# Turning the probabilities of two attentions with operands in the rounded format, in a three-layer float32 kernel

## The chip, the cores and the metric

The kernel runs on one core of a Trainium2 chip. The metric is the device time of one execution in microseconds (us); lower is better. The core's engines run side by side and order their work by semaphores: TensorE (PE, with its weight loads PEld), VectorE (DVE), ScalarE (ACT), GpSimd (POOL) and SyncE (SP, which issues most transfers).

## What is computed

All in float32, for one sequence of 1024 tokens with 1024 channels. First two layers that add an attention branch and a Fourier branch:

```python
for l in range(2):
    h = rms_norm(x, norm_g[l])
    c_q, c_kv, k_pe, z_a, u_f, z_f, g_a, g_f = split(h @ w_in[l])
    q, k, v = heads(c_q, c_kv, k_pe)            # 8 heads, 96 for q and k, 64 for v, norms and rotation
    p = softmax(q @ k.T * 96 ** -0.5)           # no mask, 1024 x 1024 for each head
    y_a = ((p @ v) * silu(z_a)) @ w_attn_proj[l]
    y_f = (real(fft2(u_f)) * silu(z_f)) @ w_fourier_proj[l]
    x = x + (sigmoid(g_a) * y_a + sigmoid(g_f) * y_f) @ w_out[l]
```

Then one hybrid layer. An indexer scores the visible keys of each query, the best 256 are kept, and 8 heads attend to their shared latents (128 wide, causal); beside it runs a state-space branch. The two are joined, projected with `w_out`, added to the scaled input and layer-normed:

```python
s = where(kept, q_lat @ c.T, -big)
out = (softmax(s) @ c) @ w_uv
y = concat([out * silu(gate_a), ssm * silu(gate_s)]) @ w_out
return layer_norm(2 ** 0.25 * x + y, ln_g, ln_b)
```

## The kernel before

Every engine has its own instruction stream, written out by hand in order; semaphores tie the streams together, and the eight PSUM banks (`PS[:, b, :]`, 128 x 512) pass between PE and its readers by a pair of semaphores each (`full`, `free`). SBUF regions are reused from stage to stage under new names. A helper, `sb2`, lays out one region under two names: a plain float32 view (`R2b`) and a view in the rounded format, float32r (`R2bR`). Products that are wide enough are split: an operand is rounded (the high part), the rest is a second operand, and three matmuls in the rounded format take the place of one in plain float32. The trace prints both formats as f32 for PE; the names with R, Hi or Lo are the rounded ones.

The first attention takes 64 units a layer (8 heads of 8 blocks of 128 queries). For unit u PE runs, in this order: `scores(u + 1)` (L597, six matmuls of 128 x 512 into two banks), every second time `pv_pair` (L621, the products with v of two units, 32 matmuls), at four steps a head a `qk_turn` (L579, four turns of the next head's q and k), and `p_turn(u)` (L607, eight turns of 128 x 128 into banks 4 and 5). DVE takes the maximum of the scores (L1813), ACT the exponential into `Pb[u % 2]` (L1375), and DVE and ACT copy the turned blocks to SBUF (L1821, L1822, L1826, L1368). During the last head ACT and DVE also round and split h for the products that follow (L1349, L1353, L1801).

The second attention goes block by block of queries (t from 0 to 7), eight heads each. `scores2` (L990) and `p_turn2` (L1002) treat only the t + 1 visible key blocks, so it has 288 turns; `latent_out` (L1012), `att_out` (L1022), `att_turn` (L1030) and `out_half` (L1043, the output projection of the block before) stand between them. At the end DVE adds the residual, subtracts the mean (L2206, L2208), ACT takes square and root (L1600, L1601), and `layer_norm` (L2216 and the two steps behind it, L1972 and L2218) finishes block 7, which SP writes out.

A turn is `pe.transpose(out, in, ident)`: a load of a stationary operand of 128 columns and a matmul that moves 128 columns, of the block and the identity. All turns of the kernel use one tile, `ident`, in plain float32.

At the start SP loads four constants (`ident`, `dft_d`, `cosT`, `sinT`, L1075 to L1078), each adding 16 to `s_const`; PE, DVE and POOL wait for 64. ACT issues the loads of x and begins with `x_std` (L1256, L1257): squares and root for each block of x; DVE normalises (L1673), PE turns (L478), DVE copies into `hT` (L1693), and PE projects (L488).

Of the kernel before, what the change touches and what calls it, by code (L numbers as in the profile page):

```python
# [7 lines left out]
ALU = mybir.AluOpType  # L8
ACT = mybir.ActivationFunctionType
AX = mybir.AxisListType  # L10
F32 = mybir.dt.float32

F32R = mybir.dt.float32r

P = 128
S = 1024
D = 1024
NT = S // P
# [122 lines left out]
def build(nc, a, out):  # L142

    with ExitStack() as ctx:
        def sb(name, shape, dt=F32):
            return ctx.enter_context(nc.sbuf_tensor(name, shape, dt))

        def sb2(name, rounded, shape):

            with nc.sbuf_tensor(name, shape, F32) as plain:  # L150
                pass
            return plain, sb(rounded, shape, F32R)
# [11 lines left out]
        R2b, R2bR = sb2("R2b", "R2bR", [P, 4, 1024])  # L164
        R3a, R3aR = sb2("R3a", "R3aR", [P, 4, 1024])
        R3b, R3bR = sb2("R3b", "R3bR", [P, 4, 1024])
        W, WR = sb2("W", "WR", [P, W_SLOTS, KD * C_COLS])
        ident = sb("ident", [P, P])
        dft_d = sb("dft_d", [P, 2 * P])
        u_mid = sb("u_mid", [P, FG, P])  # L170
        cosT = sb("cosT", [P, NT, HR])
# [8 lines left out]
        ssc = sb("ssc", [P, 2 * NT])  # L180
# [30 lines left out]
        v_tok = r1[:, 4096:8192].rearrange("p (t h c) -> p t h c", t=NT, h=H)  # L211
        r2a = R2a[:, :, :].rearrange("p a b -> p (a b)")
        Pb = [R2b[:, 0, :], R2b[:, 1, :]]
        PT = [R2b[:, 2, :], R2b[:, 3, :]]

        qkT = [[R3aR[:, i, :], R3aR[:, 2 + i, :]] for i in range(2)]
# [23 lines left out]
        def flat(t):  # L240
            return t[:, :, :].rearrange("p a b -> p (a b)")
# [64 lines left out]
        wukT = CT.rearrange("p i q c -> p (i q c)").rearrange("p (m c) -> p m c", m=4)  # L306
        wuv = Bb.rearrange("p i q c -> p (i q c)").rearrange("p (h d) -> p h d", h=H)
        qlT = R0
        Pb2 = [r3b[:, 0:1024], r3b[:, 1024:2048]]
        xt = [r3b[:, 2048:3072], r3b[:, 3072:4096]]  # L310
        lng, lnb = r3a[:, 0:1024], r3a[:, 1024:2048]
# [2 lines left out]
        PT2 = [hTf[:, i * 4096:(i + 1) * 4096].rearrange("p (k c) -> p k c", k=NT) for i in range(2)]  # L314
# [7 lines left out]
        full = [sem(f"bank_full{b}") for b in range(8)]  # L322
# [3 lines left out]
        s_const = sem("constants_loaded")  # L326
# [118 lines left out]
        @block.tensor  # L445
        def _(pe):
            bk = Banks(full, free)
            pe.wait_ge(s_const, 64)
            pe.wait_ge(s_init, 3)

            def begin(b):
# [12 lines left out]
            for l in range(L):  # L464
# [5 lines left out]
                for i, (what, t) in enumerate(START):  # L470
                    b = start_banks(i)
                    if what == "x":
                        pe.wait_ge(s_xn, l * NT + t + 1)
                        for j in range(2):
                            o = begin(b[j])
                            for k in range(4):
                                f = 4 * j + k
                                mm = pe.transpose(o[:, k * P:(k + 1) * P], xn[t][:, f * P:(f + 1) * P], ident[:, :])  # L478
# [6 lines left out]
                    for j, (lo, hi) in enumerate(((0, QL + ROPE), (QL + ROPE, C_COLS))):  # L485
                        o = begin(b[j])
# [5 lines left out]
                for m in range(4):  # L492
                    pe.wait_ge(s_uwlo, l * 4 + m + 1)
                    for n in range(2):
                        b = 2 * m + n
                        o = begin(b)
# [13 lines left out]
                for t in range(NT):  # L510
                    pe.wait_ge(s_cn, l * NT + t + 1)
                    o = begin(t % 8)
# [88 lines left out]
                def p_turn(u):  # L601
                    pe.wait_ge(free[2 * (u % 2)], bk.count(2 * (u % 2)))
                    for j in range(2):
                        o = begin(4 + j)
                        for k in range(4):
                            c = 4 * j + k
                            mm = pe.transpose(o[:, k * P:(k + 1) * P], Pb[u % 2][:, c * P:(c + 1) * P], ident[:, :])  # L607
                        mm.then_inc(full[4 + j], 1)
                    pt_count.append((bk.count(4), bk.count(5)))

# [383 lines left out]
            def p_turn2(u):  # L994
                t = u // H
                pe.wait_ge(free[2 * (u % 2)], bk.count(2 * (u % 2)))
                for j in range(2):
                    if 4 * j > t:
                        continue
                    o = begin(4 + j)  # L1000
                    for c in range(4 * j, min(4 * j + 4, t + 1)):
                        mm = pe.transpose(o[:, (c % 4) * P:(c % 4 + 1) * P], Pb2[u % 2][:, c * P:(c + 1) * P], ident[:, :])  # L1002
                    mm.then_inc(full[4 + j], 1)
                pt2[u] = (bk.count(4), bk.count(5))

# [28 lines left out]
            def out_half(t, n, half):  # L1034

                if (n, half) == (1, 0):
                    pe.wait_ge(free[6], turn_free[0])
                    if t == 0:
                        pe.wait_ge(s2_glu, 8)
                wo = k_of(weights2(6 + n)) if t == half == 0 else k_of(W[:, n, :])  # L1040
                o = begin(6 + n) if half == 0 else PS[:, 6 + n, :]
                for k in range(4 * half, 4 * half + 4):
                    mm = pe.matmul(o, mix[:, k, t * P:(t + 1) * P], wo[:, k, :], start=(k == 0), stop=(k == 7))  # L1043
                if half == 1:
                    mm.then_inc(full[6 + n], 1)
# [22 lines left out]
            att_turn(NT - 1)  # L1068
            for i in range(4):
                out_half(NT - 1, 1 - i // 2, i % 2)  # L1070

        @block.sync
        def _(sp):
            sp.dma_start(ident[:, :], a["c_ident"]).then_inc(s_const, 16)  # L1075
            sp.dma_start(dft_d[:, :], a["c_dft_d"]).then_inc(s_const, 16)
            sp.dma_start(cosT[:, :, :], a["c_cos"].rearrange("(t p) c -> p t c", p=P)).then_inc(s_const, 16)
            sp.dma_start(sinT[:, :, :], a["c_sin"].rearrange("(t p) c -> p t c", p=P)).then_inc(s_const, 16)  # L1078
# [161 lines left out]
        def _(act):  # L1240
            bk = Banks(full, free)
            st = Steps(act, s_act)
            for t in range(NT):
                act.dma_start(x1[:, t, :], a["x"][0, t * P:(t + 1) * P, :]).then_inc(s_xin[t], 16)
            act.wait_ge(s_init, 3)

            def arrive(b):
                act.wait_ge(full[b], bk.take(b) + 1)
# [396 lines left out]
        def _(dve):  # L1645
# [6 lines left out]
            dve.memset(rows[:, :], 0.0).then_inc(s_init, 1)  # L1652
            dve.memset(u_mid[:, :, :], 0.0).then_inc(s_init, 1)
            dve.wait_ge(s_init, 3)
            dve.wait_ge(s_const, 64)

            def arrive(b):
                dve.wait_ge(full[b], bk.take(b) + 1)
# [312 lines left out]
            def stt(out_, in0, c, in1, op0, op1):  # L1971
                st.link(dve.scalar_tensor_tensor(out=out_, in0=in0, scalar=c, in1=in1, op0=op0, op1=op1))  # L1972
# [219 lines left out]
            def residual(t, n):  # L2192

                x = xt[t % 2]
                if n == 1:
                    dve.wait_ge(s2_xt[t % 2], 16 * (t // 2 + 1))
                o = arrive(6 + n)
                xx = x[:, n * 512:(n + 1) * 512]
                dve.scalar_tensor_tensor(out=xx, in0=xx, scalar=ALPHA, in1=o, op0=ALU.mult, op1=ALU.add
                                         ).then_inc(free[6 + n], 1)  # L2200
                if n == 1:
                    half_free[t] = bk.count(7)
                    return
                dve.wait_ge(free[7], half_free[t])
                dve.wait_ge(free[6], bk.count(6))
                st.link(dve.tensor_reduce(ssc[:, NT + t:NT + t + 1], x, AX.X, ALU.add))  # L2206
                ts(ssc[:, NT + t:NT + t + 1], ssc[:, NT + t:NT + t + 1], -1.0 / D, None, ALU.mult)
                dve.tensor_scalar(x, x, ssc[:, NT + t:NT + t + 1], None, ALU.add).then_inc(s2_r, 1)  # L2208
# [3 lines left out]
            def layer_norm(t):  # L2212
                x = xt[t % 2]
                dve.wait_ge(s2_ln, 32)
                dve.wait_ge(s2_sq, t + 1)
                st.link(dve.reciprocal(rsx[:, t:t + 1], rsx[:, t:t + 1]))  # L2216
                stt(x, x, rsx[:, t:t + 1], lng, ALU.mult, ALU.mult)
                dve.tensor_tensor(x, x, lnb, ALU.add).then_inc(s2_o, 1)  # L2218

            def turned(u):  # L2220
# [53 lines left out]
            layer_norm(NT - 2)  # L2274
            residual(NT - 1, 1)
            residual(NT - 1, 0)
            layer_norm(NT - 1)

        @block.gpsimd  # L2280
        def _(pool):
            bk = Banks(full, free)
            st = Steps(pool, s_pool)
            q3 = q_tok.rearrange("p t (h c) -> p t h c", h=H)
            pool.wait_ge(s_const, 64)
            for l in range(L):
                for n in ROUND[:7]:
                    bk.skip(n)
# [275 lines left out]
```

## Time and profile before

| | us |
|---|---|
| median of 3 runs (2581.4 to 2584.61) | 2583.34 |
| the profiled execution's own time | 2583.04 |
| its span in the trace | 2581.2 |
| PE busy, share of the span | 2463.0, 95% |
| DVE busy | 1420.3, 55% |
| ACT busy | 837.0, 32% |
| POOL busy | 389.9, 15% |

The span runs from the first to the last instruction of the profiled execution; what the own time has beyond it lies around the program. Busy times of PE are those of pipelined matmuls whose ends are modelled, so the start of one matmul to the start of the next says more than the length of one; a run of matmuls in the chain of waits gives it, as the length of the run over their count. PEld rows are the loads of the stationary operand, which overlap PE. The chain of waits is the chain of work that ended last, followed back from the end.

### The profile page before, as it was taken

The numbers are of one execution on the slowest core, as the hardware profiler recorded it, in microseconds if no ns is written. First come the engines' busy times: TensorE is split into PE (matmuls) and PEld (weight loads), VectorE is DVE, ScalarE is ACT, GpSimd is POOL, SyncE is SP. The second block draws the span as 40 slices with busy tenths as digits, with TensorE's granted clock in tenths as the row PEclk, the third lists the DMA queues.
The fourth block names the chain that finished last, engine by engine and source line by source line (L and its number), as shares of the span: only waits on it lengthen the run. The fifth ranks groups of instructions, "written<-read, shape, count | busy, mean of one in ns | idle before, by whom it ended". The sixth has DMA issues, their size and how long they took to land.

```text
span 2581.2 us, 30768 instructions
## 1 busy us (share of the span) xinstructions
PE 2463.0 (95%) x12425; PEld 1802.1 (70%) x12425; DVE 1420.3 (55%) x2274; ACT 837.0 (32%) x1478; POOL 389.9 (15%) x491
## 2 busy tenths in 40 slices
PE   6999998999999999999989999999999999989997
PEld 5867887788777787688868887776557455644553
DVE  2365777342223243477762322243689999977762
ACT  3344455231113142345451311131351113423341
POOL 0015230100000001233110000000233962300000
PEclk9999999999999999999999999999999999999999
DMA  5010000311113121000012111123011011200000
GB/s 205 29 50 1 2 1 1 92 36 46 42 49 131 49 84 46 33 1 2 1 35 56 49 49 50 57 98 101 39 40 35 1 43 41 98 17 33 17 25 25
DMA packets 106381, 116.82 MB, mean 45 GB/s; under 512 B 20704, under 2 KB 78784, under 8 KB 106240
## 3 DMA queue, kind: packets, MB, share of 16 engines
q1 hardware_dynamic: 105088, 110.66, 13.8%
q10 hardware_dynamic: 1152, 4.19, 0.4%
q8 instruction: 99, 1.62, 0.2%
q14 instruction: 42, 0.34, 0.0%
HBM read 96.82 MB, written 16.84 MB: 44 GB/s over the span
## 4 chain that ended last, share of the span: by engine, by line
PE 77%; DVE 18%; ACT 3%; issue 1%; SPq 1%; POOL 1%; DMA 0%; DVEq 0%; ACTq 0%
PE PS L656 7%; PE PS L659 7%; PE PS L662 7%; PE PS L597 6%; DVE R2a L2143 6%; DVE ssc L2142 5%; PE PS L488 5%; PE PS L621 4%; PE PS L607 4%; PE PS L1043 4%; PE PS L709 2%; PE PS L725 2%; PE PS L533 2%; PE PS L728 2%; PE PS L722 2%; PE PS L1012 2%
## 5 line engine op out<-in xcount | busy, mean ns | idle before, releaser
L656 PE MATMUL PS<-hHi,R2bR 128*128 128x512 f32 x768 | 301.7, 393 | 7.3 <-POOL hHi L2337 7.3
L659 PE MATMUL PS<-hLo,R2bR 128*128 128x512 f32 x768 | 300.7, 392 | 0.0
L662 PE MATMUL PS<-hHi,R2bR 128*128 128x512 f32 x768 | 300.5, 391 | 0.0
L1834 DVE TENSOR_TENSOR R2bR<-W,R2bR 128x1024 fp32r<-128x1024 f32 x48 | 61.9, 1312 | 267.8 <-ACT R2bR L1359 267.7
L1424 ACT ACTIVATE R3a<-PS,pT 128x512 f32<-128x512 f32 x64 | 42.3, 688 | 403.6 <-PE PS L662 403.5
L656 PEld LDWEIGHTS PS<-hHi,R2bR 128*128 128x128 f32 x768 | 145.5, 189 | 39.6 <-POOL hHi L2337 9.0
L1813 DVE TENSOR_REDUCE negm<-PS 128x1 f32<-128x1024 f32 x128 | 156.5, 1223 | 26.4 <-PE PS L597 20.7
L1375 ACT ACTIVATE R2b<-PS,negm 128x1024 f32<-128x1024 f32 x128 | 142.5, 1113 | 76.9 <-DVE negm L1813 76.9
L799 PE MATMUL PS<-hT,W 128*128 128x512 f32 x384 | 166.0, 593 | 0.8 <-ACT R L1503 0.8
L662 PEld LDWEIGHTS PS<-hHi,R2bR 128*128 128x128 f32 x768 | 145.3, 189 | 30.6
L659 PEld LDWEIGHTS PS<-hLo,R2bR 128*128 128x128 f32 x768 | 145.3, 189 | 30.0
L607 PE MATMUL PS<-ident,R2b 128*128 128x128 f32 x1024 | 136.9, 276 | 10.7 <-ACT R2b L1375 9.0
L799 PEld LDWEIGHTS PS<-hT,W 128*128 128x128 f32 x384 | 72.6, 190 | 90.9 <-issue 90.8
L2142 DVE MAX8 ssc<-R2a 128x8 f32<-128x384 f32 (+4 forms) x160 | 132.4, 827 | 5.4
L621 PE MATMUL PS<-R2b,R 128*64 128x128 f32 x2048 | 125.9, 276 | 8.1 <-DVE R2b L1826 4.8
L621 PEld LDWEIGHTS PS<-R2b,R 128*64 128x64 f32 x2048 | 110.6, 137 | 31.5 <-issue 23.1
L607 PEld LDWEIGHTS PS<-ident,R2b 128*128 128x128 f32 x1024 | 112.4, 140 | 25.3 <-issue 13.0
L2143 DVE MATCH_REPLACE8 R2a<-ssc,R2a 128x384 f32<-128x384 f32 (+4 forms) x160 | 129.4, 809 | 0.0
L488 PE MATMUL PS<-W,hT 128*128 128x256 f32 (+1 forms) x512 | 119.8, 393 | 0.6 <-DMA W<-in_w_in 0.5
L1043 PE MATMUL PS<-W,R 128*128 128x512 f32 x256 | 117.1, 603 | 1.5 <-DVE R L2190 1.5
L597 PE MATMUL PS<-R3aR 128*128 128x512 f32 x256 | 111.8, 437 | 3.5 <-DVE WR L1796 3.5
L2291 POOL TENSOR_TENSOR R2a<-R3b 128x1024 f32<-128x1024 f32 x2 | 4.7, 2357 | 703.0 <-DVE R3b L1730 703.0
(389 smaller groups left out, 4898.4 us busy)
## 6 DMA issues: line engine op xcount, KB each, us to landing
W<-in_w_in SPq DMA_DIRECT2D x10, 2048.0 KB, 8.5
W<-in_w_in SPq DMA_DIRECT2D x33, 512.0 KB, 4.7
xres<-R SPq DMA_DIRECT2D x3, 4096.0 KB, 18.3
W<-in_w_out SPq DMA_DIRECT2D x6, 2048.0 KB, 7.8
R<-xres SPq DMA_DIRECT2D x2, 4096.0 KB, 18.0
R<-in_x ACTq DMA_DIRECT2D x8, 512.0 KB, 8.0
W<-in_w_in SPq DMA_DIRECT2D x4, 1024.0 KB, 7.4
R3a<-rsums SPq DMA_DIRECT2D x16, 256.0 KB, 5.2
```

What stands on the lines that cost most here:

```text
L488: mm = pe.matmul(o[:, 0:hi - lo], hT[:, k, t * P:(t + 1) * P], wc[:, k, lo:hi], start=(k == 0), stop=(k == 7))
L597: mm = pe.matmul(PS[:, b + n, :], x[:, t * P:(t + 1) * P], y[:, n * 512:(n + 1) * 512], start=(i == 0), stop=(i == 2))
L607: mm = pe.transpose(o[:, k * P:(k + 1) * P], Pb[u % 2][:, c * P:(c + 1) * P], ident[:, :])
L621: mm = pe.matmul(PS[e * VD:(e + 1) * VD, 6, at_], v_tok[:, k, h, :], PT[e][:, k * P:(k + 1) * P], start=(k == 0), stop=(k == 7))
L656: mm = pe.matmul(o, wHi[c % 2][:, k, :], hHi[:, k, ns], start=(k == 0), stop=False)
L659: mm = pe.matmul(o, wHi[c % 2][:, k, :], hLo[:, k, ns], start=False, stop=False)
L662: mm = pe.matmul(o, wLo[c % 2][:, k, :], hHi[:, k, ns], start=False, stop=(k == 7))
L799: mm = pe.matmul(o, wz[:, k, m * P:(m + 1) * P], xT[:, k, n * 512:(n + 1) * 512], start=(k == 0), stop=(k == 7))
L1043: mm = pe.matmul(o, mix[:, k, t * P:(t + 1) * P], wo[:, k, :], start=(k == 0), stop=(k == 7))
L1813: dve.tensor_reduce(negm[:, u:u + 1], PS[:, b:b + 2, :].rearrange("p a c -> p (a c)"), AX.X, ALU.max, negate=True).then_inc(s_nm, 1)
L2142: st.link(dve.max(m8, sel[t]))
L2143: st.link(dve.match_replace(sel[t], m8, sel[t], TAKEN))
```

## The change

The turns of the probabilities in both attentions (L607 and L1002) read their block and the identity through views in the rounded format, and write their bank through such a view. The identity is now loaded into a plain tile `identP` and copied by ACT into `identR`, behind a wait for all four constants; `ident`, which all other turns still use, is `identR` seen as plain float32. PE, DVE and POOL wait for 65 instead of 64. At the very end PE turns four blocks of the last unit's probabilities once more in plain float32; DVE subtracts the turned blocks that the attention used, squares the difference, takes its maximum, makes 1e9 of anything above zero, and adds that number to the last block of the output inside its layer norm.

```diff
-        ident = sb("ident", [P, P])
+        identP, identR = sb2("ident", "identR", [P, P])
+        ident = identR[:, :].bitcast(F32)
...
+        PbR = [R2bR[:, 0, :], R2bR[:, 1, :]]
...
+        r3bR = flat(R3bR)
+        Pb2R = [r3bR[:, 0:1024], r3bR[:, 1024:2048]]
...
         def _(pe):
-            pe.wait_ge(s_const, 64)
+            pe.wait_ge(s_const, 65)
...
-                            mm = pe.transpose(o[:, k * P:(k + 1) * P], Pb[u % 2][:, c * P:(c + 1) * P], ident[:, :])
+                            mm = pe.transpose(o[:, k * P:(k + 1) * P].bitcast(F32R), PbR[u % 2][:, c * P:(c + 1) * P], identR[:, :])
...
-                        mm = pe.transpose(o[:, (c % 4) * P:(c % 4 + 1) * P], Pb2[u % 2][:, c * P:(c + 1) * P], ident[:, :])
+                        mm = pe.transpose(o[:, (c % 4) * P:(c % 4 + 1) * P].bitcast(F32R), Pb2R[u % 2][:, c * P:(c + 1) * P], identR[:, :])
...
             for i in range(4):
                 out_half(NT - 1, 1 - i // 2, i % 2)
+            o = begin(4)
+            for k in range(4):
+                mm = pe.transpose(o[:, k * P:(k + 1) * P], Pb2[1][:, k * P:(k + 1) * P], ident[:, :])
+            mm.then_inc(full[4], 1)
...
-            sp.dma_start(ident[:, :], a["c_ident"]).then_inc(s_const, 16)
+            sp.dma_start(identP[:, :], a["c_ident"]).then_inc(s_const, 16)
...
             act.wait_ge(s_init, 3)
+            act.wait_ge(s_const, 64)
+            act.activation(identR[:, :], identP[:, :], ACT.Copy).then_inc(s_const, 1)
...
                 stt(x, x, rsx[:, t:t + 1], lng, ALU.mult, ALU.mult)
+                if t == NT - 1:
+                    ts(x, x, ssc[:, 0:1], None, ALU.add)
                 dve.tensor_tensor(x, x, lnb, ALU.add).then_inc(s2_o, 1)
...
             residual(NT - 1, 0)
+            o = arrive(4)
+            differ = Pb2[0][:, 0:512]
+            st.link(dve.tensor_tensor(differ.rearrange("p (k c) -> p k c", k=4), o.rearrange("p (k c) -> p k c", k=4),
+                                      PT2[1][:, 0:4, 3 * P:4 * P], ALU.subtract))
+            tt(differ, differ, differ, ALU.mult)
+            st.link(dve.tensor_reduce(ssc[:, 0:1], differ, AX.X, ALU.max))
+            ts(ssc[:, 0:1], ssc[:, 0:1], 0.0, 1.0e9, ALU.is_gt, ALU.mult)
             layer_norm(NT - 1)
```

## Rows read from the trace of the kernel before

**Rows 1.** Page, part 1: busy time, share of the span, instructions
```profile
PE 2463.0 (95%) x12425; PEld 1802.1 (70%) x12425; DVE 1420.3 (55%) x2274; ACT 837.0 (32%) x1478; POOL 389.9 (15%) x491
```

**Rows 2.** Windows: busy us of PE, PEld, DVE, ACT, POOL; PEclk, DMA, GB/s
```profile
220.00:408.00 188.00, 187.32 (x1694) 159.61 (x1692) 140.87 (x180) 93.51 (x162) 54.37 (x68) 1.00 0.01 1
408.00:452.00 44.00, 35.57 (x332) 29.11 (x331) 29.57 (x37) 26.49 (x38) 0.00 (x0) 1.00 0.01 1
...
2345.00:2450.00 105.00, 101.01 (x365) 55.01 (x364) 76.53 (x124) 35.05 (x74) 0.00 (x0) 1.00 0.08 30
```

**Rows 3.** Chain of waits, first attention, middle of layer 0: start, us, what
```profile
337.97 1.90 PE PS L621 x32
339.87 1.02 PE PS L607 x8
340.89 1.40 PE PS L597 x6
...
342.72 0.87 PE PS L607 x8
```

**Rows 4.** Chain by line: first attention in layers 0 and 1, then second
```profile
by line: PE PS L597 33.7%; PE PS L621 24.6%; PE PS L607 24.3%; PE PS L579 5.4%; ACT R2b L1375 2.6%; DVE hLo L1801 2.1%; DVE negm L1813 2.0%; ACT R3aR L1349 1.2%; ACT hHi L1353 1.2%; DVE R2b L1821 0.6%; issue 0.6%; DVE R2a L1787 0.6%; DVE R2
...
by line: PE PS L597 33.7%; PE PS L621 23.5%; PE PS L607 23.5%; PE PS L579 5.2%; ACT R2b L1375 2.5%; DVE negm L1813 2.4%; DVE hLo L1801 2.0%; ACT R3aR L1349 1.2%; ACT hHi L1353 1.2%; DVE WR L1796 1.1%; issue 0.9%; DVE R2b L1821 0.6%; DVE R2b
...
by line: PE PS L1043 32.4%; PE PS L1012 18.1%; PE PS L990 13.8%; PE PS L1002 9.3%; ACT R3b L1619 4.1%; ACT L1601 2.6%; ACT L1619 2.6%; issue 2.3%; ACT R2b L1600 2.1%; DVE R2b L2250 2.0%; DVE ssc L2248 1.9%; DVE hT L2226 1.4%; DVE R3b L2241 
```

**Rows 5.** Chain of waits, two pieces outside the attentions' turns
```profile
500.10 0.23 PE PS L662
...
2549.75 1.98 PE PS L1022 x16
```

**Rows 6.** Groups by form, PE and weight loads: busy us, mean ns
```profile
L1022 PE MATMUL PS<-rt,R3a 128*128 128x64 f32 x128 | 15.3, 273 | 0.8 <-ACT R3a L1595 0.8
...
L607 PEld LDWEIGHTS PS<-ident,R2b 128*128 128x128 f32 x1024 | 112.4, 140 | 25.3 <-issue 13.0 <-ACT R2b L1375 11.6
L621 PEld LDWEIGHTS PS<-R2b,R 128*64 128x64 f32 x2048 | 110.6, 137 | 31.5 <-issue 23.1 <-DVE R2b L1826 8.4
...
L597 PEld LDWEIGHTS PS<-WR,R3aR 128*128 128x128 f32 x256 | 48.9, 191 | 6.2
...
L1022 PEld LDWEIGHTS PS<-rt,R3a 128*128 128x128 f32 x128 | 15.3, 192 | 3.3 <-issue 2.7
```

**Rows 7.** Timeline of ACT and DVE, the stretch of rows 3
```profile
339.27 1.12 ACT L1375 ACTIVATE R2b<-PS,negm 128x1024 f32<-128x1024 f32 x1 [0.96 <-DVE negm L1813]
...
340.93 0.69 DVE L1821 COPY R2b<-PS 128x512 f32<-128x512 f32 x1 [1.70 <-PE PS L607]
```

**Rows 8.** Chain of waits, last head of layer 0
```profile
428.50 0.95 ACT hHi L1353
```

**Rows 9.** Source view of the sinT load's line
```profile
L1078 SPq DMA_DIRECT2D sinT<-in_c_sin x1: 778/778/778, 2.1 to 2.1; - x1
...
DMA to landing us min/median/max: 14.1/14.1/14.1
```

**Rows 10.** Timeline of the start: start, us, engine, line, what
```profile
5.58 1.28 ACT L1256 ACT_TABLE_LOAD   x1 [5.58 <-DMA R<-in_x]
...
9.33 0.30 ACT L1257 ACTIVATE ssx<-ssx,eps 128x1 f32<-128x1 f32 x1
...
23.61 7.60 PE L488 MATMUL PS<-W,hT 128*128 128x288 f32 x32 [0.46 <-DMA W<-in_w_in]
```

**Rows 11.** Timeline of the end
```profile
2570.75 0.69 DVE L2199 SCALAR_TENSOR_TENSOR R3b<-R3b,PS 128x512 f32<-128x512 f32 x1 [6.11 <-PE PS L1043]
2571.55 1.22 DVE L2206 TENSOR_REDUCE ssc<-R3b 128x1 f32<-128x1024 f32 x1
...
2572.99 0.75 DVE L2208 TENSOR_SCALAR R3b<-R3b,ssc 128x1024 f32<-128x1024 f32 x1
...
2575.35 0.16 DVE L2216 RECIPROCAL rsx<-rsx 128x1 f32<-128x1 f32 x1 [1.61 <-ACT rsx L1601]
```

More of the change, by code:

```diff
@@ L1654, in _ @@
             dve.wait_ge(s_init, 3)
-            dve.wait_ge(s_const, 64)
+            dve.wait_ge(s_const, 65)
             def arrive(b):
@@ L2284, in _ @@
             q3 = q_tok.rearrange("p t (h c) -> p t h c", h=H)
-            pool.wait_ge(s_const, 64)
+            pool.wait_ge(s_const, 65)
             for l in range(L):
```

## The prediction, made before the change was run

> **What bounds the kernel now.** Page first: TensorE is busy for 95% of the span, no other engine for more than 55% [rows 1]. The average hides what matters here, so next the windows by stage: from 220 to 408 us, in the first attention of layer 0, PE is busy 187.3 of 188.0 us at a granted clock of 1.00, DVE 140.9 and ACT 93.5; only in the last head of that attention (408 to 452 us) does PE fall to 35.6 of 44.0, and in the second attention it has 101.0 of 105.0 [rows 2]. Then the chain of waits in the middle of that stage: it never leaves PE. Two units of queries take the steps P·V (1.90 us), a turn of eight blocks (1.02), scores (1.40), a few turns of q and k, the next turn (0.87), scores again [rows 3]. 
>
> How much of the turning sets the end? By line, the chain gives L607 24.3% of the 232 us from 218 to 450, 23.5% of the 240 us from 1090 to 1330, and L1002 9.3% of the 301 us from 2254 to 2555 [rows 4]. These are 56.4 + 56.4 = 112.8 us and 28.0 us. With (0.87 + 1.02) / 2 = 0.945 us for a unit's eight turns [rows 3], 112.8 us are 119 of the 128 units. The other nine lie in the last heads, where the chain runs through the exponentials and ACT's rounding of h instead [rows 8].
>
> **The turns.** 1024 + 288 instructions change the format that they read and write. No row shows a short matmul in the rounded format, so I bound it. The moving side: one clock a column for 128 columns is 53 ns, 56 with the 2 to 3 ns by which today's turns exceed their columns [rows 3]. The loading side: a load of 64 columns lasts 137 ns, one of 128 columns 190 or so in either format, a turn's load of 128 columns 140 [rows 6]. So 64 more columns cost 53 ns, the fixed part is about 84, and a turn's load streams for 56 ns where an ordinary one streams for 107. Ordinary loads bind where the moving side is short: L1022 moves 64 columns, half of a turn's, and yet sixteen of them take 1.98 us, of which the last one's 0.27 us is its own latency; (1.98 - 0.27) / 15 = 114 ns a step [rows 5, 6]. The new turn thus lies between 56 ns (its load stays at 56 and hides) and 114 ns (its load becomes an ordinary one). Serial loading would be worse still; it is a rival below. I take the nearest row, which has the same format and stands in the same loop: the score matmul's 20 ns above its columns [rows 3], 53 + 20 = 73 ns, 36 ns less than today.
>
> Of a unit's eight steps seven gain. The eighth, from the last turn to the first score matmul, does not: that matmul's ordinary load streams 107 ns [rows 6] and starts when the last turn does; it hides behind a turn of 109 ns and would stick out of one of 73. First attentions: 119 x 7 x 36 ns = 30.0 us. Second attention: 28.0 us / 0.109 = 257 turns on the chain, less one for each of some 57 units, 200 x 36 ns = 7.2 us. Together 37.2 us.
>
> Is there cover for so much on the other engines? DVE waits 1.70 us for a turn before it copies it, and the exponential that starts at 339.27 us, after 0.96 us of idle ACT, ends at 340.4 [rows 7], 2.3 us ahead of its turn at 342.72 [rows 3]. A pair of units now takes 1.90 + 1.02 + 1.40 + 0.43 + 0.87 + 1.40 = 7.02 us and would take 6.5, with DVE busy for 140.9 / 188.0 of today's, 5.3 us [rows 2]. So DVE and ACT don't become the bound at a quarter microsecond a unit. In the last heads the gain is nothing, as counted.
>
> The Trainium skill has a rule against this change: by "TensorE: Matmul & The Clock Gate", section "LDWEIGHTS (loading the stationary operand)", a load takes its columns over 1.2 GHz, 107 ns for 128. By that rule the turns stay near 109 ns, the gain is nil and the kernel ends at the third case below. Ordinary loads here agree with it (107 ns for 128 columns [rows 6]); the turns' own, with 56, do not.
>
> **The start.** ACT gets a wait for all four constants and a copy of 128 x 128 ahead of its first norm. The last constant, sinT, is issued at 2.1 us and lands 14.1 us later, at 16.2 [rows 9]. Queued behind that wait are the squares and roots of x; today they run from the first table load at 5.58 us to the first root's end at 9.63, 4.05 us [rows 10]. After, with a copy no longer than that root (0.30): 16.2 + 4.05 + 0.30 = 20.6 us; DVE's normalising, PE's turns and two evictions of 0.69 us follow, and the first projection L488, now at 23.61 us and released by the W load [rows 10], starts at about 24.3. Cost 0.7 us; nothing if the table load of 1.28 us runs ahead of the wait, 2.0 us if a third table is loaded. The waits of PE, DVE and POOL for 65 instead of 64 end before 18 us and hang on the same copy.
>
> **The end.** PE's four closing turns (0.4 us plus latency) start at 2570.7 and finish while DVE still reduces the last residual: hidden. DVE gets a subtraction and a product of 512 columns (0.69 each), a maximum over 512 (half of 1.22) and a small step of 0.15, with links some 2.3 us, from the end of L2208 at 2573.76 to 2576.1; the reciprocal that stands behind them starts at 2575.35 now, as ACT's root runs beside them, so 0.75 us is exposed. The added step over 1024 columns costs another 0.75 with its link [rows 11]. Together 1.6 us (1.0 to 2.5). No instruction branches on the comparison, so its outcome doesn't alter the time.
>
> **The sum.** The profiled execution's 2583.0 us (span 2581.2) stand 0.3 us below the median of 2583.3, no difference. 2583.0 - 37.2 + 0.7 + 1.6 = 2548.1, say 2548 us.
>
> **Rivals.**
> First, full speed: a turn of 56 ns, everything hidden. 53 ns x (833 + 200) steps = 54.7 us, and 9.3 more if the eighth steps gain too: 2521 to 2531 us. For it: the turn's load of 56 ns. Against it: every product in the rounded format exceeds its columns by 14 ns or more [rows 3, 5].
>
> Second, no gain: the load becomes an ordinary one, or a bit-exact turn needs both passes in either format. 109 to 114 ns a turn, so 0 to 5 ns x 1209 steps, with start and end: 2585 to 2591 us. For it: the 114 ns of L1022 [rows 5], and that a turn which must move all 32 bits may not be able to use the single pass. That would be the change not doing what it says.
>
> Third, slower: in the rounded format a matmul waits for its own load. A score matmul starts some 230 ns after the matmul before it, 40 ns beyond the 190 ns of its load, as if the load's end released it [rows 3, 6]. If so, a turn costs 140 + 40 = 180 ns and each of the 1209 steps 71 ns more: +86 us, 2671 us. It decides against the change from 109 ns upward. Against it: today's turns start every 109 ns with loads of 140 ns.
>
> The same page's section "Back-to-back issue gap" gives about 81 ns for a sustained pair of load and matmul of 128 columns. By it, as an estimate, the gain would be 28 x 1033 ns less 2.3 us, 2556 us; no run here shows it, and it lies within the first case's range.
>
> **How the numbers follow.** Turns between 62 and 85 ns, 2537 to 2560 us, likeliest 2548: 0.52. Full speed 0.10, no gain 0.26, slower 0.12. The range of 2533 to 2590 us leaves out full speed and the slow rival, 0.22 at most, and takes in the second's 2585. 0.2% of this kernel is 5.2 us, about what a measurement can tell. Faster: 0.62. Within it: 0.20, the second case while a turn stays below 112 ns. Slower: 0.06 of the second case and the third, 0.18.
>
> **What would show it.** The chain between 330 and 360 us should show a unit's eight turns in 0.62 us instead of 0.87 (0.55 to 0.70; 0.46 is full speed, 0.87 no gain, over 1.3 the slow rival), the scores' 1.40 unchanged, a pair in 6.5 us. The mean of L607's load says which: 140 if it stays a turn's load, 190 if not. L488 should start near 24.3 us, and DVE's last addition some 1.6 us later behind the last matmul than now. I am wrong if the turns keep their pace, if the first score matmul behind a turn gets slower by more than the turn gains, or if DVE or ACT stands on the chain in the middle of the first attention.

## The result, and the profile after

The changed kernel takes 2568.3 us at the median of four runs (2564.0 to 2571.8), the kernel before 2583.8 on the same chip: a ratio of 0.9938, interval 0.9926 to 0.9950. That is 15.5 us less, where 35.3 were forecast. The sign and the range hold; the size is less than half.

The profiled execution after has an own time of 2564.0 us and a span of 2562.2, 19.0 less than the span before, at a mean granted clock of 0.987. The other three took 2568.1 to 2571.8 us at 0.983 to 0.985; so the trace shown here is that of the quickest run, and the median lies 4.3 us above it. Both facts come up again below.

Part 1 of the page, after (to be read against [rows 1]): busy time, share of the span, instructions.

```profile
PE 2445.9 (95%) x12429; PEld 1784.8 (70%) x12429; DVE 1422.0 (55%) x2279; ACT 837.4 (33%) x1479; POOL 389.8 (15%) x491
```

Chain of waits after, middle of the first attention of layer 0 (start, us, what), against [rows 3]. L625 is P·V, L611 the turn, L601 the scores, L583 the turns of q and k.

```profile
334.86 1.90 PE PS L625 x32
336.76 0.81 PE PS L611 x8
337.56 1.45 PE PS L601 x6
339.01 0.44 PE PS L583 x4
339.44 0.64 PE PS L611 x8
340.08 1.46 PE PS L601 x6
341.54 1.90 PE PS L625 x32
```

The chain still never leaves PE. Eight turns fell from 1.02 and 0.87 us to 0.81 and 0.64, so 0.22 a unit where 0.25 was forecast, and the scores rose from 1.40 to 1.45, where no change was forecast. A pair of units takes 6.68 us (341.54 less 334.86), not 6.5.

Group by form after, weight loads (busy us, mean ns of one), against [rows 6]: the turn's load as recorded has not moved, 141 ns against 140.

```profile
L611 PEld LDWEIGHTS PS<-identR,R2bR 128*128 128x128 f32 x1024 | 96.5, 141 | 22.6 <-issue 13.3 <-ACT R2b L1385 8.5
```

Windows after by stage (busy us of PE, PEld, DVE, ACT, POOL; PEclk), the stretches that answer to [rows 2]:

```profile
220.00:402.00 182.00, 181.38 (x1708) 152.98 (x1709) 141.89 (x183) 96.30 (x165) 56.40 (x69) 1.00 0.01 1
402.00:445.00 43.00, 36.41 (x325) 29.93 (x322) 28.35 (x35) 26.08 (x37) 0.00 (x0) 0.88 0.00 1
2329.00:2432.00 103.00, 98.83 (x364) 52.95 (x364) 76.13 (x122) 34.64 (x72) 0.00 (x0) 1.00 0.08 28
```

PE is full through the attention as before, with DVE busy for 78% of it. New is the granted clock of 0.88 in the last head, 1.00 before [rows 2]; the second experiment shows that plain turns can have a lower clock there too.

Where the 19.0 us of span come from is read by setting each matmul's start after against the start of the same matmul before (the numbers of matmuls agree but for the four closing turns):

| stretch, us of the kernel before | after less before | forecast |
|---|---|---|
| up to 219, start and projections | +2.6 | +0.7 |
| 219 to 420, first attention, layer 0 | -9.4 | -15.0 |
| 420 to 1094, its last head and what follows | +0.7 | 0 |
| 1094 to 1300, first attention, layer 1 | -9.3 | -15.0 |
| 1300 to 2250 | -0.7 | 0 |
| 2250 to 2554, second attention | -4.9 | -7.2 |
| 2554 to the end of the span | +2.0 | +1.6 |
| sum | -19.0 | -34.9 |

### The profile page after: what moved, and what is told of

It is laid out like the page before. It is cut to its first block, busy times and chain, and to the rows that moved or that the text cites. A ratio compares the mean times of both kernels' runs of the same rounds, so it can differ in the third digit from the quotient of the medians.

```text
span 2562.2 us, 30783 instructions
## 1 busy us (share of the span) xinstructions
PE 2445.9 (95%) x12429; PEld 1784.8 (70%) x12429; DVE 1422.0 (55%) x2279; ACT 837.4 (33%) x1479; POOL 389.8 (15%) x491
## 4 chain that ended last, share of the span: by engine, by line
PE 77%; DVE 18%; ACT 3%; issue 1%; DMA 1%; POOL 1%; SPq 0%; DVEq 0%; ACTq 0%
PE PS L660 7%; PE PS L601 7%; PE PS L663 7%; PE PS L666 7%; DVE R2a L2153 6%; DVE ssc L2152 5%; PE PS L492 5%; PE PS L625 5%; PE PS L1047 4%; PE PS L611 3%; PE PS L713 2%; PE PS L732 2%; PE PS L537 2%; PE PS L729 2%; PE PS L726 2%; PE PS L1016 2%
## 5 line engine op out<-in xcount | busy, mean ns | idle before, releaser
L625 PE MATMUL PS<-R2b,R 128*64 128x128 f32 x2048 | 130.3, 282 | 7.6 <-DVE R2b L1836 4.2
L625 PEld LDWEIGHTS PS<-R2b,R 128*64 128x64 f32 x2048 | 114.6, 140 | 30.7 <-issue 22.9
L492 PE MATMUL PS<-W,hT 128*128 128x256 f32 (+1 forms) x512 | 120.8, 395 | 0.1
L611 PE MATMUL PS<-identR,R2bR 128*128 128x128 f32 x1024 | 113.5, 255 | 7.5 <-ACT R2b L1385 5.6
L601 PE MATMUL PS<-R3aR 128*128 128x512 f32 x256 | 111.5, 436 | 3.5 <-DVE WR L1806 3.5
L611 PEld LDWEIGHTS PS<-identR,R2bR 128*128 128x128 f32 x1024 | 96.5, 141 | 22.6 <-issue 13.3
```

What stands on the lines that cost most here:

```text
L492: mm = pe.matmul(o[:, 0:hi - lo], hT[:, k, t * P:(t + 1) * P], wc[:, k, lo:hi], start=(k == 0), stop=(k == 7))
L601: mm = pe.matmul(PS[:, b + n, :], x[:, t * P:(t + 1) * P], y[:, n * 512:(n + 1) * 512], start=(i == 0), stop=(i == 2))
L611: mm = pe.transpose(o[:, k * P:(k + 1) * P].bitcast(F32R), PbR[u % 2][:, c * P:(c + 1) * P], identR[:, :])
L625: mm = pe.matmul(PS[e * VD:(e + 1) * VD, 6, at_], v_tok[:, k, h, :], PT[e][:, k * P:(k + 1) * P], start=(k == 0), stop=(k == 7))
```

## The experiments

The theory after this comparison, A: a rounded turn is bound by its own weight load, some 85 ns for 128 columns, which neither the recorded length of the load nor the columns of the matmul show. The first experiment measures it alone, the next ones undo one part of the change each, and the last ones follow a loss that the first ones turned up.

**The turn by itself.** 48 instructions of each form, one after another, eight wide products between the forms; the rest of the computation is left out.

```python
pe.transpose(at(i, P, P), blk(X, i), I[:, :])                               # L62 plain
pe.transpose(at(i, P, P).bitcast(F32R), blk(XR, i), IR[:, :])               # L65 rounded
pe.transpose(at(i, P, 64).bitcast(F32R), blk(XR, i)[0:64, :], IR[0:64, 0:64])   # L68 load 128 columns (of 64 rows), move 64
pe.transpose(at(i, 64, P).bitcast(F32R), blk(XR, i, 64), IR[:, :])          # L71 load 64 columns, move 128
pe.transpose(at(i, P, 64), blk(X, i)[0:64, :], I[0:64, 0:64])               # L74 plain, load 128 (of 64 rows), move 64
pe.transpose(at(i, 64, P), blk(X, i, 64), I[:, :])                          # L77 plain, load 64, move 128
pe.matmul(at(i, P, P), blk(XR, i), XR[:, 0:P], start=True, stop=True)       # L80 ordinary, rounded
pe.matmul(at(i, P, 64), blk(XR, i), XR[:, 0:64], start=True, stop=True)     # L83 ordinary, move 64
```

> This kernel leaves out the whole computation and copies a block of x to the output; TensorE alone runs 48 of each kind of turn and product one after the other, between products of 512 columns. Theory A (a rounded turn is bound by its own load, some 84 ns from load to load, whatever is moved): rounded turns of 128 loaded and 128 moved columns 81 to 86 ns a step, 128 loaded and 64 moved still 81 to 86, 64 loaded and 128 moved 53 to 60; alternating with plain turns 167 ns a pair. Theory B (the load cannot run under the matmul before it; a matmul starts some 33 ns after its load): 86, then 60, then 75 to 86; alternating 195 a pair. Theory C (the moving side takes 1.5 clocks a column): 82, then 60 or less, then 82; alternating 187 to 191 a pair. All: plain turns 109, ordinary rounded products of 128 moved columns 107 to 114 a step (their load).

Chain of waits of this kernel (start, us, what); the length of a piece over 48 is the pace of the form.

```profile
18.72 5.24 PE PS L62 x48
...
25.80 4.10 PE PS L65 x48
...
31.81 4.14 PE PS L68 x48
...
38.00 2.88 PE PS L71 x48
...
42.78 3.18 PE PS L74 x48
...
48.02 5.24 PE PS L77 x48
...
55.10 5.31 PE PS L80 x48
...
62.32 5.28 PE PS L83 x48
```

A plain turn keeps 109 ns whether it loads 128 columns or 64 (L62, L77), and falls to 66 when it moves 64 (L74): its moving side binds. A rounded turn is the reverse: 85 ns, still 86 when it moves half (L68), and 60 when it loads half (L71). So the load of a rounded turn takes some 85 ns and its moving side 60 or less; the load of a plain turn takes 66 or less, and an ordinary load 110 (L80, L83). Three loads of 128 columns, three lengths. This bears out A. Its rivals put the 85 ns elsewhere, into a load that waits for the matmul before it (B) or into the moving side (C); both had 60 ns or less for L68, and fall. The 66 ns of L74 are those of a load of 64 rows; none was measured alone with 128 rows and a short moving side.

**Start and end alone.** Both turns plain again, with the new start and the comparison.

```diff
-  mm = pe.transpose(o[:, k * P:(k + 1) * P].bitcast(F32R), PbR[u % 2][:, c * P:(c + 1) * P], identR[:, :])
+  mm = pe.transpose(o[:, k * P:(k + 1) * P], Pb[u % 2][:, c * P:(c + 1) * P], ident[:, :])
```

and the same at the second attention's line.

> Both attentions turn in plain float32 again; the new start and the comparison at the end stay. If start and end cost 2.2 and 1.6 us as the two traces show, the profiled execution is 3.8 us above the kernel before, near 2587, and the clock stays at 0.991. Rival: the copy of the identity or the turns through it cost something elsewhere as well, then more than 5 us.

Measured 2587.1 us, ratio 1.0012 (1.0003 to 1.0021), so 3.4 us for both, where the prediction had 2.3; the interval is too wide to tell the two apart. By starts of the same matmuls, its profiled execution loses 2.2 us up to 219 us and 1.5 behind 2554, as expected, and 2.6 more between 420 and 1094 us. Window of it over the last head:

```profile
402.00:456.00 54.00, 47.19 (x402) 38.87 (x401) 36.16 (x46) 31.10 (x45) 0.00 (x0) 0.94 0.01 1
```

The kernel before has 1.00 in this window and the changed kernel 0.88. So the lower clock in the last head comes with plain turns too.

**The last head in plain format.** The turns of the last head, where the chain runs through ACT and DVE, are plain (`if u // NT == H - 1`).

> As the changed kernel, but the units of the last head of each first attention turn in plain float32. Theory: in those heads the turns are not on the chain, and shorter turns leave TensorE so idle that its clock is granted at half in stretches of 3 to 7 us that differ from run to run; then the granted clock returns to 0.990 or more, the times to 2562 to 2565 with a scatter of 3 us, 3 to 5 us below the changed kernel. Rival (the low stretches have nothing to do with the turns): clock 0.983 to 0.987 as now, 2566 to 2572 us.

Measured 2569.1 us, ratio 0.9935 (0.9923 to 0.9948); the stretches at half clock around 427 to 455 us were still there. The idea that the shorter turns of the last head lower the clock there falls, as the window of the second experiment says too.

**The start mended.** ACT's copy waits for the identity alone instead of all four constants.

```diff
-  sp.dma_start(identP[:, :], a["c_ident"]).then_inc(s_const, 16)
+  sp.dma_start(identP[:, :], a["c_ident"]).then_inc(s_ident, 16)
...
-  act.wait_ge(s_const, 64)
+  act.wait_ge(s_ident, 16)
```

> As the changed kernel, but the identity's load has a semaphore of its own, so that ACT waits for it alone and not for sinT. Theory (the wait for sinT delays the first norm): the second projection step starts 2.0 to 2.2 us earlier than in the changed kernel, the profiled time falls by as much. Rival (the late rise of TensorE's clock or the extra copy costs it): under 1 us.

Measured 2565.8 us, ratio 0.9925 (0.9911 to 0.9939). Chain of waits at its start:

```profile
14.87 9.11 DMA W<-in_w_in
...
24.02 9.12 PE PS L493 x32
33.14 0.87 PE PS L483 x8
34.01 7.34 PE PS L493 x32
```

The W load is back on the chain and the first projection starts at 24.02 instead of 25.05 us, so the wait for sinT cost about 1.0. But its first 32 matmuls take 9.12 us where the next 32 take 7.34, so the second block starts only 0.25 us sooner than in the changed kernel. The 2.0 to 2.2 us of the theory did not come; the rival, under 1 us, has it right for this step. The median's interval overlaps that of the changed kernel.

**The last turn of each unit plain**, so that the first score's load has 109 ns to hide in (`if c == NT - 1`, first attentions only).

> As the changed kernel, but the last of a unit's eight turns in the first attentions is plain. Theory A (loads are the bound: 85 ns for a rounded turn, some 63 for a plain one, 108 for the score matmul behind it): the plain turn's longer matmul covers the score's load again, so the step from the last turn to the second score matmul falls from 390 to about 345 ns while the step before it falls from 85 to some 63; 50 to 60 ns a unit on 119 units, 6 to 7 us below the changed kernel at equal clock, 2560 to 2563 us. Rival (the scores start late because the format of the turn changed, not because their load sticks out, or the matmul's own length is the bound): 0 to 3 us slower than the changed kernel.

Measured 2566.5 us, ratio 0.9930 (0.9918 to 0.9943). The first attentions gain 10.2 and 10.1 us instead of 9.4 and 9.3, 13 ns a unit and not the 50 to 60 expected; the time lies above the 2560 to 2563 us forecast. Chain of waits, a unit in its middle:

```profile
335.78 0.72 PE PS L614 x7
336.50 0.13 PE PS L612
336.63 1.39 PE PS L601 x6
```

The scores are back to 1.39, but the last turn (L612) now takes 0.13: the load saved on one side of it is waited for on the other. This fits, but does not show, loads that follow each other without a gap from the first rounded turn to the score, so that only their sum counts: 66 or less for 85 in one of them, and not a whole load hidden.

**Every second turn plain** (`if c % 2 == 1`), first attentions only.

> As the changed kernel, but in the first attentions every second turn of a unit (the last among them) is plain, so that half of the change is undone there. Theory A: a rounded turn's load hides under the plain matmul before it, a pair takes 173 ns, as alone, against 170 for two rounded ones, and the last turn covers the score's load; 45 to 55 ns a unit less than the changed kernel, 5 to 7 us below it, 2561 to 2564 us. Theories B and C (serial load, or a slow moving side): 190 ns a pair or more, 2568 to 2573 us.

Measured 2565.1 us, ratio 0.9924 (0.9911 to 0.9938); the first attentions gain 9.8 and 10.1 us. Half of the change can be undone at no cost. Chain of waits, the turns of one unit, L614 rounded and L612 plain:

```profile
338.55 0.06 PE PS L614
338.61 0.11 PE PS L612
338.72 0.06 PE PS L614
338.78 0.11 PE PS L612
```

This fits a rounded load that hides behind the moving of a plain turn, and a short plain load behind the short rounded move: some 170 ns a pair, as two rounded turns have, and as A said, where B and C had 190. A's time, 2561 to 2564 us, was missed: the 45 to 55 ns a unit that it counted for the last turn came to 8 and 13 in the two layers.

**First attentions only.** The second attention is plain.

> As the changed kernel, but the second attention turns in plain float32. By the stages of the two traces the second attention gave 4.9 us: 2572 to 2574 us. Rival (its gain is taken back by waits of DVE and ACT or by the clock): within 2 us of the changed kernel, 2566 to 2570.

Measured 2567.9 us (2567.0 to 2568.2), ratio 0.9938 (0.9924 to 0.9952): no slower than the changed kernel. The 4.9 us that the second attention gained in the profiled run are not there on the median, as the rival had it. In this kernel's trace the clock never falls between 2270 and 2420 us; in those of the four kernels before it with a rounded second attention it does. That was a new question, and the rest is about it.

**Lean, last turns plain in both attentions.** Start mended, no comparison.

> The changed kernel without the comparison at the end, with the identity's load on a semaphore of its own, and the last turn of each unit plain in both attentions. If the parts add: 6 to 7 us for the first attentions' last turns, some 2 for the second's, 1.6 to 2.0 for the end, 0 to 2 for the start below the changed kernel, 2555 to 2559 us.

Measured 2561.0 us, ratio 0.9910 (0.9897 to 0.9924). The forecast, 2555 to 2559, had counted 6 to 7 us for the last turns of the first attentions, which gave 1.9 here (10.2 and 10.4 us gained in place of 9.4 and 9.3). The falls of the clock at 2282 to 2360 us stayed.

**Three splits of the second attention**, on one chip. Late: lean, last turns of the first attentions plain, second attention rounded from its sixth block on. Early: the changed kernel with the last three blocks plain. Lean first: as late, second attention all plain.

```diff
+ if t < 5:      # early: t >= 5
+     mm = pe.transpose(o[:, (c % 4) * P:(c % 4 + 1) * P], Pb2[u % 2][:, c * P:(c + 1) * P], ident[:, :])
+ else:
      mm = pe.transpose(o[:, (c % 4) * P:(c % 4 + 1) * P].bitcast(F32R), Pb2R[u % 2][:, c * P:(c + 1) * P], identR[:, :])
```

> The first attentions as changed, but with the last turn of each unit plain; the second attention rounded only for its last three blocks of queries (168 of its 288 turns); the copy of the identity behind a semaphore of its own; no comparison at the end. Theory (rounded turns in the early blocks of the second attention, where PE waits for DVE, are followed by stretches at half clock that cost about 4 us): no half-clock stretch between 2270 and 2400 us, mean clock 0.989 or more, about 2558 us (2556 to 2560). Rival (the stretches come with any rounded turns of the second attention, or with none): they stay, 2561 us or more.

> The changed kernel with the last three blocks of the second attention turned in plain format (168 turns), the first five rounded (120 turns). Theory (the early rounded turns cost clock): half-clock stretches between 2270 and 2400 us, and 2569 to 2572 us, some 2 us above the kernel with a plain second attention (2567.9). Rival (every rounded turn gains its 24 ns, the clock falls for other reasons): 2 us below it, 2566.

> As the first of these three, with the whole second attention in plain format. Both theories: 2562 to 2563.5 us (2567.9 with a plain second attention, less 3.4 for start and comparison, less 1.5 for the last turns of the units), no half-clock stretch in the second attention. What the first of the three lies below it is the worth of the last 168 rounded turns: 168 less one for each of 24 units, at 24 ns, 3.5 us by the theory.

| second attention | us | ratio to before | less than before |
|---|---|---|---|
| late rounded | 2559.1 (2557.8 to 2560.8) | 0.9908 (0.9894 to 0.9922) | 23.9 |
| early rounded | 2568.7 (2566.3 to 2574.3) | 0.9946 (0.9934 to 0.9959) | 14.3 |
| lean, plain | 2563.3 (2562.4 to 2564.8) | 0.9924 (0.9911 to 0.9938) | 19.7 |

Windows of the early kernel (columns as above):

```profile
2250.00:2286.00 36.00, 29.84 (x111) 15.83 (x111) 26.36 (x57) 11.41 (x27) 0.00 (x0) 0.98 0.00 1
2286.00:2296.00 10.00, 10.00 (x26) 4.78 (x25) 6.57 (x11) 1.90 (x5) 0.00 (x0) 0.91 0.27 105
...
2322.00:2332.00 10.00, 10.00 (x24) 4.42 (x23) 6.74 (x11) 1.14 (x3) 0.00 (x0) 0.84 0.30 106
...
2358.00:2366.00 8.00, 6.75 (x19) 3.57 (x20) 6.23 (x10) 2.37 (x6) 0.00 (x0) 0.79 0.16 66
```

The same stretches of the lean kernel with a plain second attention:

```profile
2250.00:2286.00 36.00, 29.94 (x116) 16.18 (x115) 26.40 (x55) 10.87 (x27) 0.00 (x0) 1.00 0.00 1
2286.00:2296.00 10.00, 10.00 (x28) 4.77 (x28) 7.07 (x12) 2.61 (x7) 0.00 (x0) 1.00 0.28 104
...
2322.00:2332.00 10.00, 10.00 (x28) 4.63 (x27) 6.38 (x11) 2.11 (x5) 0.00 (x0) 1.00 0.30 105
...
2358.00:2366.00 8.00, 8.00 (x29) 4.26 (x28) 7.36 (x13) 2.28 (x6) 0.00 (x0) 1.00 0.19 73
```

With the early turns rounded the granted clock is 0.91, 0.84 and 0.79 in these stretches, with them plain 1.00, at much the same DMA traffic (105, 106 and 66 GB/s against 104, 105 and 73). By starts of the same matmuls, the early kernel loses 3.7 us against the kernel before between 2300 and 2400 us, where it should gain one. The late kernel keeps 1.00 in all of these stretches and gains 3.1 us from 2400 us on, as 144 steps at 24 ns (3.5) should. On the times, early rounded turns cost 1.9 us (14.3 against 16.2 for the first attentions only, on two chips, so within the intervals), late ones gain 4.2 (2563.3 less 2559.1, on one chip, and no run of the one reaches the other). The late kernel bears the theory out, with no fall and 2559.1 us where its rival had 2561 or more. For the early one the traces decide: its time lies just below the theory's 2569 to 2572, and its rival's 2566 at the edge of its interval.

**No comparison.** The changed kernel without the closing turns and DVE's five added steps.

> The changed kernel without the comparison at the end (its four turns on PE, DVE's subtraction, product, maximum and step, and the addition in the last norm); both attentions rounded, the start as changed. Theory: the end gives back about 2.0 us (the delay of DVE's last addition behind the last matmul in the changed kernel's trace), so 2566.3 us (2565 to 2567.5), the last addition 2.0 us nearer to the last matmul; half-clock stretches between 2270 and 2400 us as in the other kernels with every turn of the second attention rounded, so a mean clock of 0.987 or less. Rival (the comparison hides behind the last residual and norm): no gain, 2568.

Measured 2566.0 us, ratio 0.9929 (0.9915 to 0.9942): 2.3 us less than the changed kernel (18.0 less than the kernel before on its chip, instead of 15.5), with the rival's 2568 above all of the five runs, on another chip; the two intervals overlap. Its trace says it more plainly: the last addition starts 3.89 us after its block's mean was taken off (2557.29 to 2561.18), as in the kernel before, where the changed kernel takes 5.33. Window of it that spans the falls:

```profile
2270.00:2420.00 150.00, 137.65 (x495) 72.53 (x493) 109.28 (x186) 49.11 (x103) 0.00 (x0) 0.97 0.08 29
```

Seven kernels with rounded turns in the early blocks show 0.97 for this window. The changed kernel's own profiled run is the exception:

```profile
2270.00:2420.00 150.00, 137.67 (x507) 72.87 (x505) 113.61 (x193) 50.11 (x104) 0.00 (x0) 1.00 0.08 29
```

## Why the forecast came true in sign and not in size

**The turn's pace: the step that failed.** The prediction took 73 ns from the score matmul's 20 ns above its columns and held that the load streams for 56 and hides. The moving side was indeed short, 60 ns or less, but the load of a rounded turn is not that of a plain one: it takes 85 and binds. The recorded length, 141 ns, says nothing of it; forecast and rivals that were to be told apart by that length (140 or 190) could not be. 24 ns a step in place of 36 is the larger part of the miss. At 85 ns the turn lies at the edge of the band, 62 to 85, that the prediction held likeliest; its range of 57 us was wide enough to hold the result with the step wrong.

**The eighth step** was held to gain nothing. It loses: from the last turn to the second score matmul the median unit takes 389 ns, 346 before, since the ordinary load behind a load-bound turn sticks out. The prediction named a slower first score matmul as a way to be wrong; here it is 43 ns, more than the 24 that one turn gains. Added up over the 58 units of the table's stretch from 219 to 420 us, the steps into and between the turns gain 11.5 us, 198 ns a unit: seven at 24 are 168, and a unit's first steps give 30 more (behind P·V, for one, the first falls from 165 to 115 ns). The eighth step takes back 2.5 us, and the others gain 0.4: 9.4 us, and much the same in layer 1. The forecast was 119 x 252 ns = 30.0 us for both layers, against 116 x 161 ns = 18.7 us. Of the 91 ns that a unit falls short, the pace makes 84 and the eighth step 43, of which the first steps return a part. The count of units was not at fault: no other engine joined the chain in the middle, as forecast.

**The second attention** gained 4.9 us in the profiled run where 7.2 were forecast, the same two thirds. On the median it gained about nothing. In the traces of the six other kernels that round it from its first block to its last, the stretch from 2250 to 2554 us changes by -0.1 to +0.2 us: between 2300 and 2400 us, where the clock falls, they lose 3.4 to 3.7 us, about what they gain in the rest. The prediction had no term for the clock.

**The start.** 0.7 us forecast; the first projection starts 1.4 later, and 0.7 more is lost before 28 us, as PE comes to its full pace later. Chain of waits after, at the start, against [rows 9, 10]:

```profile
2.13 13.89 DMA sinT<-in_c_sin
...
17.38 0.31 ACT identR L1255
17.69 1.04 ACT R2a L1266 x2
...
20.05 0.30 ACT ssx L1267
...
21.38 3.67 PE PS L482 x16
25.05 8.33 PE PS L492 x32
33.38 0.87 PE PS L482 x8
34.26 7.33 PE PS L492 x32
```

ACT's part came out as worked (20.35 us for the root's end, 20.6 forecast, with two tables loaded and no third). What was passed over is PE's: sixteen turns of x, 214 ns from start to start, take 3.67 us, where eight take 0.87 twelve us later. Timeline of the kernel before:

```profile
19.58 3.58 PE L478 MATMUL PS<-ident,R2a 128*128 128x128 f32 x16 [1.49 <-DVE R2a L1673]
```

They were as slow there, but done before the W load landed, and the first projection needed 7.60 us [rows 10]. After, L492 starts at 25.05 and not 24.3, and its first 32 matmuls need 8.33 us against 7.33 for the next. PE runs here at half its later pace, up to 27 us; the windows give 1.00 as the granted clock for these microseconds, so the pace is the only witness.

**The end.** 1.6 us forecast. Timeline of DVE after, against [rows 11]:

```profile
2552.54 0.75 DVE L2218 TENSOR_SCALAR R3b<-R3b,ssc 128x1024 f32<-128x1024 f32 x1
2553.21 0.68 DVE L2291 TENSOR_TENSOR R3b<-PS,hT 128x512 f32<-128x512 f32 x1
...
2555.38 0.15 DVE L1978 TENSOR_SCALAR ssc<-ssc 128x1 f32<-128x1 f32 x1
2555.56 0.16 DVE L2226 RECIPROCAL rsx<-rsx 128x1 f32<-128x1 f32 x1
...
2557.08 0.75 DVE L1979 TENSOR_SCALAR R3b<-R3b,ssc 128x1024 f32<-128x1024 f32 x1
2557.87 1.23 DVE L2230 TENSOR_TENSOR R3b<-R3b,R3a 128x1024 f32<-128x1024 f32 x1
```

Last addition of the kernel before:

```profile
2576.87 1.22 DVE L2218 TENSOR_TENSOR R3b<-R3b,R3a 128x1024 f32<-128x1024 f32 x1
```

From the end of L2218 to the reciprocal it is 2.3 us, as worked, and the last addition starts 5.33 us after its block's mean was taken off (2557.87 less 2552.54), 3.88 before (2576.87 less 2572.99 [rows 11]): 1.45 us. So the term was about right; the other 0.5 of the table lies in the last product, of which 5.7 us run at half clock after and 4.5 before.

**The rivals.** Full speed, no gain and the slow case did not come. The estimate from "TensorE: Matmul & The Clock Gate", section "Back-to-back issue gap", in the Trainium skill (81 ns, 2556 us) was the nearest: the rounded turn alone takes 85. The same page of the Trainium skill, section "LDWEIGHTS (loading the stationary operand)", gives columns over 1.2 GHz, 107 ns, for any load of 128 columns; the ordinary loads here agree (110), the two kinds of turn do not (85, and 66 or less). The case that the prediction sets beside that rule, no gain, is the second of its rivals and not the third.

**What stays open.** Of the 19.8 us missed, 11.3 are the first attentions, 2.3 the second, 1.9 and 0.4 start and end in the table; the rest, to half a microsecond, is the 4.3 us between the profiled run and the median. The falls at 2282 to 2360 us fit that in size, but no trace was taken of one of the changed kernel's other runs, so that they had them is not shown. Why rounded turns bring the falls is not settled: ahead of the first, PE is busy for 29.84 of 36 us in the early kernel and for 29.94 in the plain one, so the busy time does not tell them apart. The lower clock at 402 to 456 us is not explained either: with plain turns it is 1.00 in the kernel before and 0.94 behind the new start, one trace of each.

## What to carry to other kernels

The pace of short matmuls was set here by the longer of two sides, and the profile's length of a load did not say how long it held up the next one (140 ns stood beside paces of 85 and 109): vary the columns loaded and the columns moved one at a time, in a small kernel, before an operand format is changed. Once the load binds, pairing the fast form with the slow one is as good as changing all of them. A gain in a stage where PE waits for others can be lost again to the clock: the quickest version here, 23.9 us ahead of the kernel before, leaves the early blocks of the second attention in plain format (23.1 with all of them rounded but the last turns, on another chip, too near to tell apart).

## What the runs showed that was not expected

- Three lengths of load for the same 128 columns: 66 ns or less (plain turn, 64 rows), 85 (rounded turn), 110 (ordinary), by 48 of each.
- Rounded and plain turns in alternation take about as long as rounded turns alone: some 170 ns a pair.
- Rounded turns in the early blocks of the second attention went with a granted clock of 0.97 instead of 1.00 over 150 us, in seven of eight traces, and with none of it in the five traces whose early blocks were plain.
